# A decoder step on one core: router picks by ranks, token turns split three and three, no unread product, the dense flag read one step earlier

## What is computed

```python
g_prob = softmax(t @ rg_w + rg_b)                  # 4 groups
g_val, g_idx = top_k(g_prob, 1)
e_logits = (t @ re_w + re_b).reshape(-1, 4, 4)     # 4 experts in each group
e_logits = take_along_axis(e_logits, g_idx)        # those of the chosen group
e_val, e_idx = top_k(softmax(e_logits), 2)
weights = g_val * e_val / sum(e_val)
combine = sum(one_hot(g_idx * 4 + e_idx, 16) * weights)
h1 = einsum('td,edf->tef', t, w1)
h3 = einsum('td,edf->tef', t, w3)
y = einsum('tef,efd->td', silu(h1) * h3 * combine, w2)
```

## Time and profile before

| | |
|---|---|
| median of 3 runs | 955.27 us (954.39 to 957.06) |
| the profiled execution: device time | 959.82 us |
| its span, first to last instruction | 957.9 us |
| TensorE busy | 902.0 us, 94% of the span |
| VectorE, ScalarE busy | 318.7 us, 173.2 us |
| moved by DMA | 316.22 MB, mean 330 GB/s |
| chain that ended last | TensorE 71%, SyncE's queue 10%, DMA 9%, VectorE 6% |

### The profile page before, as it was taken

One profiled execution on the slowest core, in us unless ns is written; L12 is line 12 of the kernel. 1 busy time (PEld: TensorE's weight loads), 2 busy tenths in 40 slices (PEclk: granted clock), 3 DMA queues, 4 the chain that ended last, 5 costly groups with the idle time before them and its releaser, 6 DMA issues.

```text
span 957.9 us, 13146 instructions
## 1 busy us (share of the span) xinstructions
PE 902.0 (94%) x5368; PEld 495.5 (52%) x5368; DVE 318.7 (33%) x797; ACT 173.2 (18%) x385; POOL 40.3 (4%) x68
## 2 busy tenths in 40 slices
PE   6999999999789899999999889999989999999985
PEld 3565665454556644444445367776654444443524
DVE  3232125446523621112110177367461111111015
ACT  3200000022312221001111040182131111011103
POOL 0000000004200000000000210000000000000020
PEclk9999999999999999999999999999999999999999
DMA  9976887789968479999999986243849999999991
GB/s 375 421 285 263 326 315 265 323 296 370 368 264 362 165 300 413 423 420 422 421 422 421 368 344 243 88 170 111 340 177 373 411 422 422 422 422 422 421 349 58
DMA packets 48151, 316.22 MB, mean 330 GB/s; under 512 B 5618, under 2 KB 6018, under 8 KB 12882
## 3 DMA queue, kind: packets, MB, share of 16 engines
q1 hardware_dynamic: 39600, 288.90, 74.5%
q0 software_dynamic: 6480, 22.30, 6.4%
q10 hardware_dynamic: 2002, 4.08, 1.2%
HBM read 303.84 MB, written 11.42 MB: 329 GB/s over the span
## 4 chain that ended last, share of the span: by engine, by line
PE 71%; SPq 10%; DMA 9%; DVE 6%; issue 2%; ACT 1%; POOL 0%; DVEq 0%; POOLq 0%
PE banks L828 26%; PE banks L1456 14%; SPq L423 10%; PE banks L1501 7%; PE banks L1415 6%; DMA ring<-in_ew 6%; PE banks L905 4%; DMA ring<-in_w 2%; PE banks L892 2%; PE banks L945 1%; PE banks L837 1%; PE banks L969 1%; DMA scr<-yd,row_i 1%; PE banks L1434 1%; PE banks L1487 1%
## 5 line engine op out<-in xcount | busy, mean ns | idle before, releaser
L828 PE MATMUL banks<-uT,ring 128*128 128x320 f32 x448 | 124.5, 438 | 2.6 <-DVE uT L1711 2.6
L1456 PE MATMUL banks<-ring,scr 128*64 128x512 f32 x512 | 113.2, 593 | 2.1 <-issue 1.8
L828 PEld LDWEIGHTS banks<-uT,ring 128*128 128x128 f32 x448 | 85.4, 192 | 42.6 <-issue 7.4
L1415 PEld LDWEIGHTS banks<-scr 128*128 128x128 f32 (+1 forms) x768 | 75.3, 190 | 14.5 <-issue 12.3
L1415 PE MATMUL banks<-scr 128*128 128x128 f32 (+1 forms) x768 | 81.4, 280 | 0.0
L1456 PE MATMUL banks<-scr 128*64 128x512 f32 x352 | 78.1, 593 | 3.4 <-DMA scr<-in_ew 3.4
L1456 PEld LDWEIGHTS banks<-ring,scr 128*64 128x64 f32 x512 | 37.4, 137 | 75.2 <-issue 74.0
L625 ACT ACTIVATE scr<-banks,mods 128x128 f32<-128x128 f32 x128 | 36.6, 368 | 172.1 <-PE banks L1415 172.1
L1934 DVE TENSOR_TENSOR scr<-scr,banks 128x512 f32<-128x512 f32 x16 | 11.0, 688 | 156.3 <-ACT scr L611 156.3
L1501 PE MATMUL banks<-scr,uT 128*64 128x512 f32 x256 | 57.1, 596 | 0.0
L828 PE MATMUL banks<-ring,uT 128*128 128x512 f32 x128 | 57.1, 599 | 0.0
(11 more groups left out here) (380 smaller groups left out, 912.2 us busy)
## 6 DMA issues: line engine op xcount, KB each, us to landing
ring<-in_ew SPq DMA_DIRECT2D x112, 1024.0 KB, 21.5
ring<-in_w SPq DMA_DIRECT2D x80, 1024.0 KB, 9.1
scr<-in_ew SPq DMA_DIRECT2D x80, 1024.0 KB, 19.0
scr<-in_v POOLq DMA_DIRECT2D x16, 256.0 KB, 9.8
yd<-uT POOLq DMA_DIRECT2D x8, 512.0 KB, 8.7
scr<-in_kT POOLq DMA_DIRECT2D x13, 256.0 KB, 6.7
out_hgrn<-scr SPq DMA_DIRECT2D x2, 1152.0 KB, 8.0
scr<-in_s POOLq DMA_DIRECT2D x1, 2048.0 KB, 11.4
```

What stands on the lines that cost most here:

```text
L828: last = mm(out, a, b, start=(first and i == 0), stop=(final and i == len(pairs) - 1))
L1415: ins = mm(ps[h][:, PAIR * j:PAIR * j + PAIR], utok[r, t, P * d:P * d + P], pick[r, t, :, :].rearrange("p e n -> p (e n)"), start=first, s ...
L1456: ins = mm(ps[bank][SLOTS * x:SLOTS * x + SLOTS, :], xe[:, kk, SLOTS * x:SLOTS * x + SLOTS], wab[SLOT[n]][:, x, kk % 4, :], start=(kk == 0 ...
```

## The change

It has four parts.

1. **Ranks.** `top1` and its tables go. `ranks` compares the four numbers of each row with one another: six comparisons write, for each number, three ones or zeros (does the other beat it), and two sums over them give each number's rank. The group of rank 0 times the two experts of rank below 2 is `sel`. A small constant `real` masks the token rows that don't exist. The one-hots and the gaps for the softmax, which `router` made on the way, are made later by the new `gaps`, after the first `pick`.
2. **Turns.** The six turns run in the order 4, 5, 0, then the positions, then 2, 1, 3. VectorE copies 4 and 5 right after `sel`, ahead of the positions. `utok_ev` counts ScalarE's four copies alone, and the gather's first half waits for two of them, the second for four. Turns 1 and 2 change banks.
3. **The unread products** of `idle(2)` go.
4. **The flag.** TensorE waits for `over_i` and reads it ahead of `first_half`, the branch stays behind it.

The core of the diff (L numbers aside, the rest is names of tiles and constants):

```diff
-        TOKEN_BANK = (0, 1, 2, 3, 7, 5)
+        TOKEN_BANK = (0, 2, 1, 3, 7, 5)
+        TURNS = (4, 5, 0, 2, 1, 3)
...
                 e.wait_ge(sem("rexp_in"), 2 * l + 1)
-                for n in range(4):
+                for n in TURNS[2:]:
                     t, c = n // 2, slice(512 * (n % 2), 512 * (n % 2) + 512)
-                    e.wait_ge(sem("utok_ps"), 6 * l + n + 1)
+                    e.wait_ge(sem("utok_ps"), 6 * l + TURNS.index(n) + 1)
...
                 lr_turn(l)
-                for n in range(4):
+                for n in TURNS[:3]:
                     tokens(l, n)
                 pe.wait_ge(sem("sel_ready"), l + 1)
...
                 last.then_inc(sem("pos_ps"), 1)
-                for n in range(4, 6):
+                for n in TURNS[3:]:
                     tokens(l, n)
-                idle(2)
...
                 if half == 0:
                     pe.wait_ge(sem(f"pick_ready{l}"), q + 1)
-                    if q == 0:
-                        pe.wait_ge(sem("utok_ev"), 6 * l + 6)
+                if q == 0:
+                    pe.wait_ge(sem("utok_ev"), 4 * l + 2 * half + 2)
...
                 gather(l, 0, 1)
-                first_half(l)
                 pe.wait_ge(sem("over_ready"), 2 * l + 1)
                 over = pe.value_load(over_i[0:1, 0:1], min_val=0, max_val=T)
+                first_half(l)
                 before = list(gone)
                 with pe.If(over > 0):
...
+            def ranks():
+
+                x = lg.rearrange("p t (g e) -> p (t g) e", e=EPG)
+                y = beats.rearrange("p t (g e) k -> p (t g) e k", e=EPG)
+                for j in range(1, EPG):
+                    tt(y[:, :, j, 0:j], x[:, :, 0:j], x[:, :, j:j + 1].broadcast_to([P, TT * 5, j]), GE)
+                for j in range(EPG - 1):
+                    last = tt(y[:, :, j, j:EPG - 1], x[:, :, j + 1:EPG], x[:, :, j:j + 1].broadcast_to([P, TT * 5, EPG - 1 - j]), ALU.is_gt)
+                step(last)
+                v.tensor_reduce(rank_g, beats[:, :, 0:EPG, :], AX, ADD)
+                step(v.tensor_reduce(rank_e, beats[:, :, EPG:5 * EPG, :], AX, ADD))
...
-                top1(lg5, best1, eq5, code1, oh1)
-                v.memset(oh1[64:P, 2, 0, :], 0.0)
-                step(stt(lg2, oh1[:, :, 1:5, :], FAR, lg5[:, :, 1:5, :], MUL, ADD))
-                top1(lg2, best2, eq5[:, :, 0:4, :], code2, oh2)
-                step(tt(lg2, oh1[:, :, 1:5, :], oh2, ADD))
-                tt(sel.rearrange("p t (g e) -> p t g e", e=EPG), lg2, over(oh1[:, :, 0, :], EPG, 3), MUL).then_inc(sem("sel_ready"), 1)
+                ranks()
+                step(stt(own_g, rank_g, 0.0, over(real, GROUPS), EQ, MUL))
+                stt(sel.rearrange("p t (g e) -> p (t g) e", e=EPG), rank_e.rearrange("p t (g e) -> p (t g) e", e=EPG), 2.0,
+                    over(own_g.rearrange("p t g -> p (t g)"), EPG), ALU.is_lt, MUL).then_inc(sem("sel_ready"), 1)
+
+            def gaps():
+
+                ts(oh1, rank, 0.0, None, EQ)
+                ts(oh2, rank, 1.0, None, EQ)
+                step(v.tensor_reduce(best1, lg5, AX, MAX))
+                step(stt(lg2, oh1, FAR, lg5[:, :, 1:5, :], MUL, ADD))
+                step(v.tensor_reduce(best2, lg2, AX, MAX))
                 tt(rx[:, :, 0:4], lg5[:, :, 0, :], best1[:, :, 0:1].broadcast_to([P, TT, 4]), SUB)
                 tt(rx[:, :, 4:8], best2, best1[:, :, 1:5], SUB).then_inc(sem("rexp_in"), 1)
...
             def slots(l):
 
+                for n in TURNS[:2]:
+                    tokens(l, n)
                 v.wait_ge(sem("sel_ready"), l + 1)
...
                 picks(l, 0)
-                for n in range(4, 6):
-                    tokens(l, n)
+                gaps()
                 counts = ps[6][:, TT * NE:TT * NE + NE]
```

More of the change, by code:

```diff
@@ L157 @@
 K_SQ = K_ML + 256
-K_RANK = K_SQ + NS_SEQ
-K_TRI = K_RANK + 4
+K_TRI = K_SQ + NS_SEQ
 K_IOTA = K_TRI + P
@@ L319, in build @@
         rt = carve(64, TT, 96)
-        best1, code1, best2, code2 = rt[:, :, 0:5], rt[:, :, 5:10], rt[:, :, 10:14], rt[:, :, 14:18]
-        eq5, oh1, oh2 = (rt[:, :, a:a + n].rearrange("p t (g e) -> p t g e", e=EPG) for a, n in ((20, 20), (40, 20), (60, 16)))
+        best1, best2 = rt[:, :, 0:5], rt[:, :, 10:14]
+        oh1, oh2 = (rt[:, :, a:a + 16].rearrange("p t (g e) -> p t g e", e=EPG) for a in (40, 60))
+        beats = carve(1088, TT, 5 * EPG, EPG - 1)
+        rank_g, rank_e, own_g = carve(1268, TT, GROUPS), carve(1280, TT, NE), carve(1328, TT, GROUPS)
+        rank = rank_e.rearrange("p t (g e) -> p t g e", e=EPG)
+        real = stat[:, 32:35]
         lg2 = rt[:, :, 76:92].rearrange("p t (g e) -> p t g e", e=EPG)
@@ L1381, in tokens @@
                 last.then_inc(sem("utok_ps"), 1)
-            def idle(n):
-                for _ in range(n):
-                    give(mm(ps[4][:, :], ident, const[:, 0:512], start=True, stop=True))
             def slots(l):
                 lr_turn(l)
-                for n in range(4):
+                for n in TURNS[:3]:
                     tokens(l, n)
@@ L1759, in tokens @@
                     v.wait_ge(sem("bias_ev"), 4 + 2 * l)
-                v.wait_ge(sem("utok_ps"), 6 * l + n + 1)
+                v.wait_ge(sem("utok_ps"), 6 * l + TURNS.index(n) + 1)
                 r = half_rows(n % 2)
-                stt(utok[r, t, c], ps[TOKEN_BANK[n]][r, :], rcol[r, t:t + 1], shifts[r, c], MUL, ADD)\
-                    .then_inc(sem("utok_ev"), 1)
-            def top1(src, best, eq, c, oh):
-                n = best.shape[2]
-                step(v.tensor_reduce(best, src, AX, MAX))
-                step(tt(eq, src, over(best, 4, 3), GE))
-                step(tt(eq, eq, const[:, K_RANK:K_RANK + 4].unsqueeze(1).unsqueeze(1).broadcast_to([P, TT, n, 4]), MUL))
-                step(v.tensor_reduce(c, eq, AX, MAX))
-                step(tt(oh, eq, over(c, 4, 3), EQ))
+                stt(utok[r, t, c], ps[TOKEN_BANK[n]][r, :], rcol[r, t:t + 1], shifts[r, c], MUL, ADD)
+            def ranks():
[8 more added lines that the diff above has]
+                step(v.tensor_reduce(rank_e, beats[:, :, EPG:5 * EPG, :], AX, ADD))
             def router(l):
@@ L1802, in combine @@
                 tt(oh2, oh2, over(e, EPG, 3), MUL)
-                step(tt(rx[:, :, 18:22], rx[:, :, 18:22], oh1[:, :, 0, :], MUL))
-                step(tt(oh2, oh2, oh1[:, :, 1:5, :], ADD))
+                step(tt(rx[:, :, 18:22], rx[:, :, 18:22], own_g, MUL))
+                step(tt(oh2, oh2, oh1, ADD))
                 for t in range(TT):
@@ L2031, in dense @@
                         gained(n + 1, i)
+            step(v.memset(real, 1.0))
+            v.memset(real[64:P, 2:3], 0.0)
             v.wait_ge(sem("const_in"), 16)
@@ L2553, in shape_constants @@
     K[:, K_SQ:K_SQ + 4] = tok[:, None] // S_LEN % 4 == np.arange(4)
-    K[:, K_RANK:K_RANK + 4] = [4, 3, 2, 1]
     K[:, K_TRI:K_TRI + P] = row < np.arange(P)[None, :]
```

## The result

The changed kernel takes 950.3 us (median of 11 runs, 947.94 to 953.79), the kernel before beside it 955.95 (11 runs): ratio 0.9933, 95% interval 0.9914 to 0.9952. It is faster, by 5.65 us where 11.7 were forecast. The profiled execution has a span of 948.0 us.

A forecast was written before the change was run, and what follows sets the result against it. The weight stream bounds each layer, restarted by TensorE's products behind the branch. Gains of 6.0 us (layer 0) and 5.7 (layer 1), together 11.7, taken from 955.27 give 943.6 us; range 941 to 949, own range 941.5 to 946.

The forecast's parts named there:

- the range: Whole kernel: time between 941 and 949 us, with 941.5 to 946 for the forecast's own case.
- What bounds it: Each layer's end: weight stream restarts with TensorE's products behind the branch; gains ahead reach the end, gains behind are worth nothing.
- The picking: VectorE's picking in each layer: 1.58 us in place of 3.26, a gain of 1.68.
- the sum: Gains per layer: 5.2 + 0.8 = 6.0 in layer 0, 5.2 + 0.5 = 5.7 in layer 1, together 11.7 us.
- the waiting pace: Dear case for VectorE's six comparisons: each starts 0.25 us after the one before, making the picking 2.36 us.
- The turns and the positions: TensorE between picking and gather: TensorE waits 1.2 us for `sel` in place of 2.87; the turns gain 0.92 us.
- The unread products: TensorE ahead of the gather, each layer: removing them gains 2.61 us, freed by moving VectorE's copies ahead of the positions.
- the clock rival: Under the gather: half-speed clock for 3.4 us costs 1.7 us of work in each layer, 947.0 us; chance 0.12.
- The flag: Read ahead of `first_half`: wins 0.8 of 1.06 us idle in layer 0, 0.5 of 0.73 in layer 1.
- what was to show it: Signs in the profile, among them idle of 0.3 us or less behind `first_half`, then all as before to each layer's end.
- a sign of being wrong: Behind the restart of the weight stream: a DMA share below 1 would show the prediction wrong.

The follow-up runs named there:

- place_probe: The changed kernel with 61 never-run products in layer 0's dense path and 31 in layer 1's; 947.92 us, ratio 0.9917 to the kernel before.
- old_picks: The changed kernel with two never-run products in layer 0's dense path and the old `top1` and `router` picking back; 949.97 us, ratio 0.9938.
- before_flag: The kernel before with only the flag's read moved ahead of `first_half`; 956.48 us, ratio 0.9988.
- idle_back: The changed kernel with the two unread 512-column products back behind the last turn in both layers; 948.34 us, ratio 0.9925.
- plus2_again: The kernel of `place_plus2` run once more, as base for later runs beside it; 948.45 us, ratio 0.9906.
- place_plus2: The changed kernel with two products that never run in layer 0's dense path, moving the code behind the branch; 945.95 us, ratio 0.9862.
- filler_place: The changed kernel with three unread products in TensorE's wait for the picks and 63 never-run products in layer 0's dense path; 945.71 us, ratio 0.9876.
- fill_one: The changed kernel with one unread 256-column product in TensorE's wait and one never-run product in layer 0's dense path; 944.74 us, ratio 0.9872.
- before_fill: The kernel before with seven unread products in its wait for the picks and 57 never-run products in layer 0's dense path; 953.46 us, ratio 0.9956.
- turn_mm: The changed kernel, two never-run products included, with the five transposed token turns written as products with the identity; 949.03 us, ratio 0.9911.

## Why the prediction was right and wrong

The direction was right, and so were the steps up to the branch; the size was twice what came, and the time lay above the range.

- **What bounds it: right, with one exception.** What TensorE gains ahead of the branch reaches the stream. In layer 1 products and restart of SyncE's queue both come 4.25 us earlier against the first comparison (15.80 behind it; before, 719.57 less 699.52, 20.05), and the last piece 5.4. Over all 17 profiles, from the first packet behind the gap to the end of the 39 pieces (81.8 MB, from the packets of the trace, less the last twelve of 9,984) are 203.3 to 205.0 us in the 30 stretches without a stall. In the four with one they are 205.5 to 206.1 (the twelve take 0.9 to 4.1 us more, and with them the two kinds overlap: 205.5 to 208.4, and 206.6 to 208.5). So counted, what TensorE loses just behind the branch the stream loses in part too, while for the prediction nothing behind that point counted. That is how layer 0 kept little of the 3.2 us at its restart. The clock's fall behind the stall isn't needed for it: `place_probe`, without that fall, has 205.9.
- **The picking: right.** 1.58 forecast, 1.60 measured; 3.4 us for both layers in the sum, 3.6 to 4.9 in `old_picks`. The six comparisons took 0.75 from the first to the sums (forecast 0.72). With each comparison at the waiting pace the picking would have been 2.36, by the prediction's estimate; the trace goes against it.
- **The turns and the positions: right in layer 0 as a sum.** Gather 4.52 behind the first comparison (forecast 4.59). TensorE waits 0.91 in place of the 1.2 foreseen. The 0.92 for the turns, though, was read from a row at half clock; at full clock the new division saves 1.34 us in a layer (4.21 less 2.87), and it is VectorE's copies that it no longer waits for.
- **The unread products: mis-sized.** 2.61 a layer was a row that lay in part at half clock. At full clock they take 1.72, and their return costs 2.0 to 3.2 us in all, where the sum has 5.2. The rest of that row was the clock's, which the change does not remove: it fell in layer 1 all the same. That was the clock rival, come true in one layer, at 0.93 us between positions and gather (3.80 from the positions' start where layer 0 had 2.87) and half a us of the gather. The 3.4 us at half speed that the rival reckons with are in the trace of before (0.50 from 325.6 to 329.0), and layer 1 of the change has as many (0.50 from 699.7 to 703.1).
- **The flag: right in its own price.** `before_flag` shortens the idle time by 0.78 and 0.52 us (1.06 to 0.28, and 0.73 to 0.21), for 0.8 and 0.5. By itself that gives nothing that can be measured in the time: 0.9988, interval 0.996 to 1.0016, which holds a gain of 1.3 us as well as none.
- **The step that failed** stands in the sum and in what was to show it: that the idle time between `first_half` and the products behind the branch would be 0.3 us or less, and that from there all would be as before. The idle time moved one row on and grew to 2.37. Removing `idle(2)` shortened the code ahead of layer 0's branch by eight instructions, at four a product, and that put a block's end behind the branch's target; `idle_back`, with the products back, has no stall there. Without the stall the change gains 9.5 to 10.0 us (`plus2_again`, `place_plus2`) in place of 5.65: it cost 3.9 to 4.4 us. Behind the restart the DMA share fell below 1 (0.74 from 342.46 to 344.46), which the prediction had named as a sign of being wrong; no rival of it named the cause.

So of 11.7 us 9.5 to 10.0 come without the stall, 3.9 to 4.4 of them are lost to it, and about 2 never came, which is the size of the unread products' excess (2.61 less 1.72, in two layers 1.8). With the wait filled on both sides and no stall, `filler_place` and `fill_one` are 7.8 and 8.7 us below `before_fill`. The 1 to 2 us more that the unfilled kernels differ by may be a clock that falls less often after the change (a mean of 0.990, before 0.986); no run shows that by itself.

## What to carry to other kernels

After every edit ahead of a branch, also in the path that doesn't run, look at the first rows behind it: here 2.35 to 2.90 us of "issue" behind row 1 were a matter of the code's place, and eight instructions that never run took them away, which tells such a stall from a stall of data. Price what an edit removes at the clock that it will have: the row of 2.61 us, in a stretch with a granted clock of 0.66, held the clock's loss, and only 1.72 of it was the products'; in layer 1 the clock fell all the same, behind a wait of 0.83 us. Filling the wait of 0.8 to 0.9 us ahead of the positions with products that nobody reads was worth 2 to 4 us here. Elsewhere, run it both ways, and several times: the runs of one kernel lay up to 8.5 us apart, as far as the gains.

## What the hardware showed

- A taken branch took TensorE's sequencer 3.3 to 3.9 us in the 17 profiles, in `turn_mm` once 4.88, with two packets of the instruction queue in it, the later 2.25 us long; what set the longer one is open.
- In all 34 passages of the branch a 16,384-byte packet of the instruction queue started 0.8 to 1.6 us into it, and the next 0.7 to 1.2 us after its end.
- With a block's end, by the count above, one row behind the branch TensorE had 2.35 to 2.90 us of idle time, 1.18 with seven rows ahead of it, and 0.08 with twelve. After the idle time the clock fell in all three kernels that had it at row one, and not in the one that had it at row seven.
- One unread product of 256 columns (0.60 us) in a wait of 0.9 us kept the clock up like three: 0.39 to 0.49 us of the wait were left.
- Runs of one kernel spread over 8.5 us (`place_plus2`) along with their mean clocks, and the profiles show falls of it that come or not in a handful of places; in the three versions of the change with the wait filled alone, it was 3 to 4 us.
